# One more wait ahead of the token gathers at the end of a two-block transformer kernel

## The reference

```
def expert_block(args):
    xb, e = args
    return (jax.nn.silu(xb @ w_gate[e]) * (xb @ w_up[e])) @ w_down[e]

ys = lax.map(expert_block, (xs, blk_e)).reshape(P, D)
y = jnp.zeros((T, D), ys.dtype).at[row_tok].add(ys * row_w[:, None].astype(ys.dtype))
...
x = x + hier_moe(rmsnorm_2(x, norm2_g[l]), ...)
```

## Time and profile before

| what | us |
|---|---|
| median of 3 runs | 1962.94 (1962.23 to 1963.41) |
| the profiled execution's own time | 1962.45 |
| its span, from the first to the last instruction | 1960.7 |
| PE busy in the span | 1832.3 (93%) |
| DVE, ACT, POOL busy | 595.0, 336.8, 18.7 |
| granted TensorE clock, mean | 0.971 of full speed |

### The profile page before, as it was taken

The page is one execution under the profiler, slowest core; times in us unless marked ns, Lnnn a source line. Parts: engine busy times, 40 slices in busy tenths (PEclk is TensorE's granted clock), DMA queues, the critical chain, the costliest instruction groups (busy, mean ns, idle before and its releaser), DMA issues.

```text
span 1960.7 us, 17259 instructions
## 1 busy us (share of the span) xinstructions
PE 1832.3 (93%) x6730; PEld 885.7 (45%) x6730; DVE 595.0 (30%) x1357; ACT 336.8 (17%) x682; POOL 18.7 (1%) x39
## 2 busy tenths in 40 slices
PE   6999899989999999989899978899969999999997
PEld 2445544434444444435344444444445554554552
DVE  3322436442222210021676332331142111111113
ACT  1111223221111110010233422331120000000000
POOL 0001000000000000000000000000000000000001
PEclk9999979999999999999899989999979999999999
DMA  9675020012221112132111101022329999999998
GB/s 392 240 274 201 4 86 1 24 38 86 86 86 63 66 65 89 59 132 90 60 43 43 43 1 43 1 91 81 129 87 374 429 429 429 428 430 429 428 429 338
DMA packets 30984, 335.42 MB, mean 171 GB/s; under 512 B 3192, under 2 KB 5768, under 8 KB 11600
## 3 DMA queue, kind: packets, MB, share of 16 engines
q1 hardware_dynamic: 23216, 310.56, 39.0%
q10 hardware_dynamic: 5168, 14.91, 2.0%
q0 software_dynamic: 2544, 9.18, 1.3%
HBM read 319.66 MB, written 18.37 MB: 172 GB/s over the span
## 4 chain that ended last, share of the span: by engine, by line
PE 84%; DMA 6%; DVE 6%; ACT 3%; issue 1%; POOL 0%; DVEq 0%; SPq 0%; ACTq 0%; POOLq 0%
PE bank L915 16%; PE bank L1248 13%; PE bank L556 10%; PE bank L574 8%; PE bank L1257 5%; PE bank L1037 5%; PE bank L1006 3%; PE bank L1045 3%; PE bank L735 2%; PE bank L632 2%; PE bank L655 2%; PE bank L877 2%; DMA arena<-in_w_expert_up 2%; DMA slot<-in_w_expert_up 2%; DMA upper<-in_w_expert_up 2%; PE bank L996 2%
## 5 line engine op out<-in xcount | busy, mean ns | idle before, releaser
L915 PE MATMUL bank<-hT,slot 128*128 128x512 f32 x704 | 304.0, 595 | 6.9 <-ACT hT L2052 6.9
L1248 PE MATMUL bank<-slot,arena 128*64 128x512 f32 x704 | 231.5, 594 | 8.8 <-DMA upper<-in_w_expert_up 5.8
L915 PEld LDWEIGHTS bank<-hT,slot 128*128 128x128 f32 x704 | 134.3, 191 | 176.6 <-issue 175.1
L1248 PE MATMUL bank<-upper,arena 128*64 128x512 f32 x352 | 154.7, 594 | 3.9 <-DMA arena<-in_w_expert_up 3.9
L556 PE MATMUL bank<-arena,slot 128*128 128x512 f32 x352 | 152.9, 597 | 3.3 <-DVE arena L1669 3.3
L1257 PE MATMUL bank<-arena 128*128 128x128 f32 x1024 | 123.2, 280 | 14.9 <-issue 14.9
L1037 PE MATMUL bank<-hT,slot 128*128 128x512 f32 x256 | 120.8, 620 | 12.0 <-ACT arena L2052 10.4
L1257 PEld LDWEIGHTS bank<-arena 128*128 128x128 f32 x1024 | 118.9, 195 | 27.2 <-issue 27.2
L574 PE MATMUL bank<-hT,slot 128*128 128x512 f32 x272 | 122.5, 608 | 7.6 <-DVE hT L1699 6.5
L1248 PEld LDWEIGHTS bank<-slot,arena 128*64 128x64 f32 x704 | 72.0, 137 | 108.7 <-issue 101.3
L556 PEld LDWEIGHTS bank<-arena,slot 128*128 128x128 f32 x352 | 67.4, 192 | 88.7 <-issue 84.7
(11 more groups left out here) (368 smaller groups left out, 1966.1 us busy)
## 6 DMA issues: line engine op xcount, KB each, us to landing
slot<-in_w_expert_gate SPq DMA_DIRECT2D x17, 2048.0 KB, 26.6
slot<-in_w_expert_down SPq DMA_DIRECT2D x16, 2048.0 KB, 30.2
slot<-in_w_in SPq DMA_DIRECT2D x15, 2048.0 KB, 8.8
slot<-in_w_ada SPq DMA_DIRECT2D x12, 2048.0 KB, 14.5
slot<-in_w_up SPq DMA_DIRECT2D x11, 2048.0 KB, 7.7
slot<-in_w_expert_up SPq DMA_DIRECT2D x11, 2048.0 KB, 25.4
upper<-in_w_expert_up SPq DMA_DIRECT2D x11, 2048.0 KB, 27.0
upper<-in_w_expert_down SPq DMA_DIRECT2D x6, 2048.0 KB
```

Of the source, the lines that this page charges most:

```text
L915: ins = pe.matmul(bank[4 * j + c][:, :], w[:, k, half:half + P], hT[:, k, :], start=(k == 0), stop=(k == KD - 1))
L1248: ins = pe.matmul(dst[b * CAP:(b + 1) * CAP, :], lhs(b, k), rhs(b, k), start=(k == 0), stop=(k == n_k - 1))
```

## The change

GpSimd gets one more wait before its first gather: it waits also until TensorE has signalled the up products of the last pair (`uu_full` at 16).

```diff
             if on("end"):
                 po.wait_ge(S["zeroed"], 16 * (ROWS - (E - 2) * CAP) // P)
                 po.wait_ge(S["y_st"], 16 * (E // 2 - 1))
+                po.wait_ge(S["uu_full"], E // 2)
                 for t in range(NT):
                     for b in range(2):
                         po.indirect_dma_start(ws[7 + b][:, t * D:(t + 1) * D], None, ys_d,
                                               bass.IndirectOffsetOnAxis(ap=slot_i[:, b * NT + t:b * NT + t + 1], axis=0))\
                           .then_inc(gath[t], 16)
```

## The result

The changed kernel takes 1966.13 us (median of 20 runs, 1963.81 to 1967.11) against 1962.64 us for the kernel before (20 runs, 1961.1 to 1963.86). That is +3.5 us, a ratio of 1.0017 with a 95% interval of 1.0010 to 1.0023. The change stays just under the 0.2% that the prediction took as its bound for "same", but it is clear of the noise and beyond the range's upper end of 1965.0. The forecast of a shift of 0.04 us was wrong. One execution of a later kernel ("half the delay") took 6090.71 us, where its other ten took 1961 to 1965; nothing on record says why, and its ratio leaves it out.

The account below looks back on a forecast made before the run. VectorE's first weighted add, waiting for token tile 0's gathers, was taken as the bound. A 4.27 us later start and a lag shrinking from 7.74 to about 3.5 us cancel: 1962.94 + 0.04 = 1963.0 us, range 1961.7 to 1965.0.

Parts of the forecast that it names:

- What bounds the kernel: Last 30 us: VectorE's first weighted add, once both gathers of token tile 0 land (1941.31), sets the time.
- The later start of the gathers: GpSimd's first gather, held by the new wait, starts at 1936.50, 4.27 us later.
- The queue in front of the gathers: DMA engines before the gathers: slab traffic gone, second gather's issue to VectorE's start shrinks from 7.74 to about 3.5 us.
- second way: Second gather's lag from the 128 KB transfers: 2.42 us fixed plus 1.27 makes 3.69 us, VectorE starts at 1941.53.
- the two 128 KB transfers: GpSimd's own mid-kernel transfers, issued at 950.25 and 950.78, landing 2.3 us after issue; taken as nearest uncontended rows.
- The bound of that lag: VectorE's start shifts between -1.2 us and, with the contended 7.74 us lag, +4.27 us; forecast at the low side.
- The later gathers: Gathers after the first pair: the last lands with 0.6 us of slack, no new break in VectorE's row.
- TensorE: Down products at the end: slabs land sooner, at most 1.56 us gained, worth nothing at the end.
- The slack of 1.8 us at the last product: TensorE's last final product is early by 1.8 us for VectorE's PSUM adds.
- The delay passes whole: Rival at the gathers: the lag is the gather's own, everything 4.27 us later, 1967.2 us; chance 0.07 (whole or most).
- VectorE and GpSimd get in each other's way: Rival at the last four gathers: issues held by VectorE's weighted adds, +4.5 us, 1967.4 us; chance 0.05.

Follow-up runs that it names:

- half the delay: The kernel before, with four memsets on GpSimd between the last store's landing and the first gather: 1962.92 us against 1962.81, ratio 0.9999.
- later wait: The changed kernel with its added wait on the last pair's turned activations (ht_full), 1.5 us after the up products: 1966.97 us, ratio 1.0021.
- held adds: The changed kernel, with VectorE waiting for all eight gathers before its first weighted add: 1974.21 us.
- no slabs: The kernel before, without the added wait and without loading the last pair's two down slabs (4 MB less): 1959.51 us, ratio 0.9982.

## Why the prediction was wrong

**What bounds the kernel: right.** The end hangs on VectorE's first weighted add. All shifts of the first add appear at the PSUM adds, with breaks on top.

**The later start of the gathers: right.** Forecast 0.80 us after D (1936.50 against 1935.70), measured 0.79 and 0.81.

**The queue in front of the gathers that goes: the step that failed,** in the size of one term. The queue did go; what was left of the lag was sized too small. The lag of the second gather into idle engines was put at 3.5 us and is 5.24 and 5.69 in the changed kernel, at most 5.45 without the slabs and 5.34 with the later wait. Both signs that the prediction had named for being wrong appeared: the first add after 1943, and in one trace breaks. Delay and lag were to cancel to +0.04 us; the first add came 1.8 and 2.2 us later after D. The 3.5 us took 1.27 us for 512 KB at 412 GB/s, the rate of gathers behind a backlog. With the 0.97 us of issue and the 0.5 us to the first byte taken off, 3.7 and 4.2 us are left in the two traces of the changed kernel. One more term of the sum was no cost: the 0.6 us from landing to VectorE measured 0.02. The prediction's second way did without it, so its two ways did not end at the same event, and their agreement was luck.

The idle start was taken from the two 128 KB transfers, and from them only the time to the first byte, which held roughly (0.5 us after the issue against 0.7: bytes from 1.7 us after an issue of 1.03). What I passed over stands in the same stretch: with a share of 0.42 those transfers moved 98 GB/s. Full engines would be 233 GB/s by that row, where full engines elsewhere moved 426. The stretches that follow in the kernel before say the same:

```profile
951.50:952.00 0.50, 0.50 (x3) 0.26 (x2) 0.50 (x1) 0.00 (x0) 0.00 (x0) 1.00 0.82 180
952.00:952.50 0.50, 0.50 (x3) 0.26 (x2) 0.50 (x1) 0.42 (x1) 0.00 (x0) 1.00 0.96 246
```

So the trace of the kernel before already had transfers into idle engines that ran slowly for their share.

By the fit of the Trainium skill, "DMA: Bandwidth & Descriptors", section "Anatomy of one DMA", a transfer of 512 KB takes an estimated 3.2 us. The changed kernel with a semaphore for each gather shows the first gather's own time, with the second issued 1.34 us behind it:

```profile
1936.83 1.04 POOL L2473 DMA_INDIRECT hT<-ys_d,smi  x1 [984.84 <-PE bank L1249]
1941.23 1.28 DVE L2043 SCALAR_TENSOR_TENSOR arena<-hT,small,arena 128x1024 f32<-128x1024 f32 x1 [4.51 <-DMA hT<-ys_d,smi]
```

It is 4.40 us to the add. The fit held for 128 KB and not here, and the measurement decides.

**The bound of that lag: placed wrongly.** I gave the cases between 3.5 and 7.7 us almost no chance, because the uncontended rows seemed the nearest in kind. They were plain copies of a quarter of the size, and the gap between the ends was 4 us. The range's upper end, 1965.0 or +2.1 us, allowed a lag of about 5.5 us, which is what came at the first add. It left no room for breaks behind it or for the 1 us by which the medians exceed the traces. With both ends of the lag open the range should have reached close to the whole delay, +4.27 us.

**The later gathers: half right.** A pair each 2.55 us and no break was forecast; one changed trace has breaks of 0.53 and 0.40 us, the other none.

**TensorE: right.** The slabs land sooner, by 0.7 us where at most 1.56 was allowed, and it is worth nothing at the end. The slack of 1.8 us at the last product fits what came later. With the adds 1.2 us sooner and the clock at 1.00 VectorE never waited for TensorE; with the adds 1.4 us sooner and the final products 1.7 us later after D than before (13.16 us against 11.47), by the lowered clock, it did.

**The rivals.** "The delay passes whole" named the right place. Its price of 4.27 us was too high and the truth lies between it and the forecast: 2.2 to 2.6 us by the traces, 3.5 by the medians. "VectorE and GpSimd get in each other's way" happens and costs nothing that the runs show; my evidence against it was one gather that had begun before the add, see below.

## What to carry to other kernels

Holding back one stream so that another has the transfers to itself pays only if the favoured one is waited for at the end. Here the slabs were early, and the gathers, which set the end, had used the tail of the slabs' traffic to hide their own start: 1.8 us later was free, 4.3 us later was not. Issue transfers while the engines are still at work, and price a transfer into idle engines from a row of the same kind and size, or keep the whole gap as the range.

## What the runs showed of the hardware that was not expected

**A GpSimd gather issued during a weighted add ends 0.81 to 0.82 us after that add.** In the changed kernel's second trace:

```profile
1943.87 1.53 POOL L2469 DMA_INDIRECT hT<-ys_d,smi  x1 [0.31 <-issue]
1945.70 1.02 POOL L2469 DMA_INDIRECT xT<-ys_d,smi  x1 [0.30 <-issue]
```

The add under way at 1943.87 began at 1943.31 and ended at 1944.59; the issue ended at 1945.40. The one under way at 1945.70 began at 1944.62 and ended at 1945.90; the issue ended at 1946.72. The two held issues of the first trace fit too (1947.11 after an add's end at 1946.30, 1948.44 after 1947.62), and with no adds beside them all from the third on take 0.94 us. Over all the traces 17 gathers were issued during a weighted add, and all 17 ended 0.81 to 0.82 us after it. A gather that began before the add was not held (0.94 us at 1941.05, the add at 1941.31), which is why the kernel before showed nothing. Nor is a gather held by the gate-by-up product, which has one of its inputs in PSUM (0.94 us at 1936.09 in the kernel before, the product from 1935.70 to 1936.39). The Trainium skill, "SBUF — State Buffer", section "Who interferes with whom", says that a VectorE instruction with two SBUF inputs contends with a GpSimd instruction that reads SBUF, and that the order of issue decides who blocks. The traces agree where the add comes first. In the other order they show no block: the add at 1941.31 took its 1.28 us beside the gather, and so did one that began 0.09 us after a gather (1943.72 and 1943.63, in the changed kernel with a semaphore for each gather).

**Gathers into idle DMA engines start slowly.** They show a high share and few bytes: share 0.87 to 0.93 with 251 to 267 GB/s in the first 2.3 us of traffic in four kernels (changed, held adds, later wait, no slabs), against 0.99 with 410 beside the slabs. Within them the first microsecond is the worst: 123 and 90 GB/s in its halves in the second trace of the changed kernel, 147 and 57 in the first. Whether the extra time is in fetching descriptors, in reading scattered rows or in something else was not tried.
